# Delta-rule matrices at 64 columns a chunk instead of 128 a pair of chunks, in a 1-core Trainium2 kernel

## Chip, cores and metric

One NeuronCore of a Trainium2 chip runs the whole program. The metric is the device time of one execution in microseconds (us); smaller is better. TensorE is also called PE here, VectorE DVE, ScalarE ACT, GpSimd POOL, SyncE SP.

## What is computed

Two blocks of two layers each on 256 tokens of width 1024, all float32. The change lies in the second block, in its gated delta-rule branch. Its core, cut from the reference (CHUNK is 64, 8 heads, dk = dv = 128):

```python
qc, kc, vc, bc, gc = (chunks(t) for t in (q, k, v, beta, g))
gc = jnp.cumsum(gc, axis=-1)
incl = pos[:, None] >= pos[None, :]
strict = pos[:, None] > pos[None, :]
diff = gc[..., :, None] - gc[..., None, :]
decay = jnp.where(incl, jnp.exp(jnp.where(incl, diff, 0.0)), 0.0)
kb = kc * bc[..., None]
m = jnp.where(strict, jnp.einsum('bnhid,bnhjd->bnhij', kb, kc) * decay, 0.0)
rhs = jnp.concatenate([vc * bc[..., None], kb * jnp.exp(gc)[..., None]], axis=-1)
sol = lax.linalg.triangular_solve(m, rhs, left_side=True, lower=True, unit_diagonal=True)
u, w = sol[..., :dv], sol[..., dv:]
a_qk = jnp.einsum('bnhid,bnhjd->bnhij', qc, kc) * decay

def step(state, xs):
    qd, kd, a, uu, ww, cd = xs
    v_new = uu - ww @ state
    o = qd @ state + a @ v_new
    state = state * cd + kd.T @ v_new
    return state, o
```

(The last function is shown with its einsums as products.) Everything else, the other branches, the gates, the feed-forward layers and the first block, is as before in both kernels.

## The kernel before

**The stream.** All weights pass through one stream (class Stream). SP loads them in 1 MB chunks, ACT rounds a half chunk to its high part (L339), POOL subtracts to get the low part (L348), and PE multiplies in three passes (L147 to L149): high by high, low by high, high by low. With activations as the moving operand a pass is 128x128 weights by 256 columns. `main.pe(pe, pos)` issues the stream up to a position; one position is half of a half chunk, that is 12 passes.

**The branch work between.** Everything that is no stream is put on PE by hand, at a position of the stream. `places` (L1541) gives the steps of the delta rule their positions: most stand 1 position apart, some 2. Each engine goes through the same list of steps in its own order and waits on semaphores. The branch is done in two halves of four heads (`hf`), in each of the two layers, so each step occurs four times. Around it DVE does the short convolutions of the next projections (L1384) in the first half, and rotations (L1582 to L1585) in the second.

**The squares.** The 256 tokens are four chunks of 64. Before the change, two chunks of a head make one 128x128 square (tt = 0, 1 names the pair), block-diagonal after masking, so 4 heads x 2 pairs = 8 squares (NP) make one tile of 128x8x128 each: `e` (decays), `es`, `at` (query by key), `mt` (the matrix m, turned), `ti` (the inverse, turned), `t` (the inverse), `y`. Several share one place in memory. In the records a tile goes by the first name at its place: `y` shows as `es`, `t` as `e`, `w` as `kb`, `u` as `vb`.

**The steps**, in order, for one half of the heads:
- spread: `spread` (L1670) puts the row of g for each head on all 128 partitions by a product with 8-row weights, 256 columns (L1672); DVE takes the difference with the token's own g into `e` (L2205), ACT takes the exponential. `spread_e` and, later, `beta` spread two more rows.
- k0, k1, v0, v1: turns of k and v (L1678), read by DVE into `kb`, `kd`, `vb`.
- q0, q1, g0, g1: `gram` (L1684) makes the products of q and k, and of k and k, 4 per step; DVE masks them into `at` and `mt`, and begins the inverse in `ti` (L2252 to L2256).
- lower0, lower1: PE turns the 8 squares of `ti` (L1732), ACT copies them into `t` (L1980).
- y1, c1 to y5, c5: the inverse by doubling. `y` is 8 products mt x t (L1739), masked by DVE with the level's mask (L2275). `c` is 8 products ti x y into yd (L1748, not in level 5) and 8 products y x ti into cp (L1749); DVE subtracts them from `ti` (L2282) and `t` (L2284). The 8 squares go in two groups g of four, each with its own PSUM bank, wait and semaphore.
- solved: u = ti x vb (L1756) and w = kb x ti (L1757), 8 products each, copied by DVE (L2290) and ACT (L1985).
- w0, o0 to w3, o3: the scan over the four chunks (L1774, L1785, L1791, L1794), in which weights of 64 columns or 64 rows already occur.

Elsewhere in the kernel, products with operands on one half of the partitions stand in L565 (first block: 64x64 weights, four groups that alternate between the two halves of partitions, in and out), L1815 (index scores: 64-row weights, heads that alternate between the halves), L534 (64-column weights, outputs that alternate) and L1606 (turns of 8 rows: 8 moving columns).

Of the kernel before, what the change touches and what calls it, by code (L numbers as in the profile page):

```python
# [56 lines left out]
def columns(spec):  # L57
    at, out = 0, {}
    for name, n in spec:
# [10 lines left out]
                   ("chunk_causal", 2 * 256), ("perm128", 128), ("freq", 2), ("levels", 6 * 128), ("upper", 128),  # L70
                   ("strict", 128), ("level0T", 128),
# [6 lines left out]
def constants():  # L78
# [40 lines left out]
    i, j = p[:, None], p[None, :]  # L119
    lev = [((i // (2 * b) == j // (2 * b)) & (i // b > j // b)) for b in (1, 2, 4, 8, 16, 32)]  # L120
    put("levels", np.stack(lev, 1).astype(np.float64))
    put("level0T", lev[0].T.astype(np.float64))
    same = i // CH == j // CH
    put("upper", (same & (j >= i)).astype(np.float64))
    put("strict", (same & (j > i)).astype(np.float64))
# [937 lines left out]
NP = 8  # L1063
LAYOUT_2 = (["sm"] + [f"{n}{i}" for h in range(2) for n in "qkvz" for i in (2 * h, 2 * h + 1)]
# [256 lines left out]
class Mixer2:  # L1321
# [342 lines left out]
    def prepare_pe(self, pe, hf):  # L1664
# [28 lines left out]
        spread(m["rowq"][:, 1, :], 0).then_inc(*sig.up("spread_g", l, hf))  # L1693
# [23 lines left out]
        spread(m["rowq"][:, 0, :], 2).then_inc(*sig.up("spread_b", l, hf))  # L1717
# [5 lines left out]
    def solve_pe(self, pe, hf):  # L1723
# [27 lines left out]
        main.pe(pe, self.step_at(hf, "solved"))  # L1751
        for g in range(2):
            pe.wait_ge(*sig.at("kept", l, hf, g, 5))
            for n in range(4 * g, 4 * g + 4):
                c = slice((n % 4) * P, (n % 4 + 1) * P)
                pe.matmul(yd[g][:, c], h["ti"][:, n, :], h["vb"][:, n, :], start=True, stop=True)  # L1756
                mm = pe.matmul(cp[g][:, c], h["kb"][:, n, :], h["ti"][:, n, :], start=True, stop=True)  # L1757
            mm.then_inc(*sig.up("solved", l, hf, g))

    def scan_pe(self, pe, hf, key_sum):  # L1760
# [4 lines left out]
        for c in range(NCH):  # L1765
# [27 lines left out]
            for hh in range(4):  # L1793
                mm = pe.matmul(op[r, hh * P:(hh + 1) * P], h["at"][r, tt * 4 + hh, r], h["vn"][r, hh, :],  # L1794
# [175 lines left out]
    def chain_act(self, act, hf, key_log):  # L1970
# [6 lines left out]
        for g in range(2):  # L1977
            main.act(act, self.step_at(hf, f"lower{g}"))
            act.wait_ge(*sig.at("begun_turned", l, hf, g))
            act.activation(h["t"][:, 4 * g:4 * g + 4, :], bank[g][:, :].rearrange("p (n i) -> p n i", n=4), ACT.Copy  # L1980
                           ).then_inc(*sig.up("t_begun", l, hf, g))
# [211 lines left out]
    def prepare_dve(self, dve, hf, unit_key):  # L2193
# [9 lines left out]
        for hh in range(4):  # L2203
            for tt in range(TT):
                ins = dve.tensor_scalar(h["e"][:, tt * 4 + hh, :], bank[hh // 2][:, (hh % 2) * T + tt * P:(hh % 2) * T + (tt + 1) * P],  # L2205
# [15 lines left out]

        for tt in range(TT):
# [11 lines left out]
        step(dve.tensor_tensor(h["e"][:, :, :], h["e"][:, :, :], K("upper").unsqueeze(1).to_broadcast([P, NP, P]), ALU.mult))  # L2234
        for tt in range(TT):
# [3 lines left out]
            dve.tensor_tensor(h["at"][:, pr, :], heads(tt), h["e"][:, pr, :], ALU.mult).then_inc(*sig.up("at_made", l, hf, tt))  # L2239
        step(dve.tensor_tensor(h["es"][:, :, :], h["e"][:, :, :], K("strict").unsqueeze(1).to_broadcast([P, NP, P]), ALU.mult))  # L2240
# [3 lines left out]
        for i in range(2):  # L2244
            ins = dve.tensor_tensor(es[:, 2 * i:2 * i + 2, :, :], es[:, 2 * i:2 * i + 2, :, :],
                                    bank[2 + i][:, :].rearrange("p (hh tt i) -> p hh tt i", hh=2, tt=TT), ALU.mult)
        step(ins)
        for tt in range(TT):
# [3 lines left out]
            dve.tensor_tensor(h["mt"][:, pr, :], heads(tt), h["es"][:, pr, :], ALU.mult).then_inc(*sig.up("mt_made", l, hf, tt))  # L2252
            dve.wait_ge(*sig.at("mt_made", l, hf, tt))
            step(dve.tensor_tensor(h["ti"][:, pr, :], h["mt"][:, pr, :], K("level0T").unsqueeze(1).to_broadcast([P, 4, P]),
                                   ALU.mult))
            dve.tensor_tensor(h["ti"][:, pr, :], K("ident").unsqueeze(1).to_broadcast([P, 4, P]), h["ti"][:, pr, :],  # L2256
                              ALU.subtract).then_inc(*sig.up("begun", l, hf, tt))

    def solve_dve(self, dve, hf):
# [3 lines left out]
        ident = K("ident").unsqueeze(1).to_broadcast([P, 4, P])  # L2263
        lev = K("levels").rearrange("p (l i) -> p l i", l=6)

        def four(b):
            return bank[b][:, :].rearrange("p (n i) -> p n i", n=4)
# [435 lines left out]
```

## Time and profile before

| | us |
|---|---|
| median of 3 runs | 2276.24 |
| lowest, highest | 2274.07, 2278.8 |
| the profiled execution | 2277.58 |
| its span, first to last instruction | 2275.8 |

Over the span, VectorE is busy 955.9 us, ScalarE 1073.0, GpSimd 1498.6, and the mean granted clock of TensorE is 0.972 of full speed. TensorE has 15336 passes and as many weight loads. The page gives for each engine the busy time, its share and the number of instructions; the timeline lists instructions in order, merged where the same ones follow each other.

### The profile page before, as it was taken

How to read it: one execution, taken by the hardware profiler on the slowest of the kernel's cores; microseconds unless marked ns; L12 is line 12 of the kernel's file. 1: busy time of each engine (PE TensorE's matmuls, PEld its weight loads, DVE VectorE, ACT ScalarE, POOL GpSimd, SP SyncE). 2: the span in 40 equal slices, each digit the busy share in tenths (PEclk: the TensorE clock that was granted, in tenths of full speed). 3: DMA queues.
4: the chain of work that ended last, by engine and by line, in shares of the span. 5: the costliest groups of instructions: out<-in, count | busy, mean ns of one | idle time of the engine just before them, and what ended most of it. 6: DMA issues, size and time to landing. Idle time of an engine off the chain costs nothing.

```text
span 2275.8 us, 35984 instructions
## 1 busy us (share of the span) xinstructions
PE 2163.2 (95%) x15336; PEld 2001.3 (88%) x15336; DVE 955.9 (42%) x1484; ACT 1073.0 (47%) x1517; POOL 1498.6 (66%) x632
## 2 busy tenths in 40 slices
PE   8989989899969899999999899998999999999998
PEld 7789978799959888989999899898889899998998
DVE  4353256442375537477112211456374681123112
ACT  4555555555545352255444444473441454544444
POOL 6679877698846234356778688663243566786886
PEclk9999999999989999999999999999999999999999
DMA  8345544355524113134445455442131344454553
GB/s 338 132 146 204 185 139 161 117 180 187 184 84 147 60 71 106 64 128 167 151 164 185 148 185 185 156 145 90 56 112 56 130 148 149 157 182 150 184 185 133
DMA packets 47183, 333.05 MB, mean 146 GB/s; under 512 B 5168, under 2 KB 5552, under 8 KB 7856
## 3 DMA queue, kind: packets, MB, share of 16 engines
q1 hardware_dynamic: 47024, 330.76, 41.9%
q8 instruction: 121, 1.98, 0.4%
q14 instruction: 38, 0.31, 0.0%
HBM read 329.69 MB, written 1.05 MB: 145 GB/s over the span
## 4 chain that ended last, share of the span: by engine, by line
PE 62%; DVE 8%; issue 1%; ACT 1%; POOL 0%; DVEq 0%; ACTq 0%
PE bank L147 14%; PE bank L149 14%; PE bank L148 14%; PE y L147 2%; PE y L149 2%; PE y L148 2%; PE bank L1749 2%; PE bank L1748 1%; PE bank L1739 1%; DVE conv L1384 1%; PE bank L1672 1%; PE bank L1794 1%; PE bank L1791 1%; PE bank L1774 1%; DVE sq L1583 1%
## 5 line engine op out<-in xcount | busy, mean ns | idle before, releaser
L348 POOL TENSOR_TENSOR w_lo<-w_raw,w_hi 128x1024 fp32r<-128x1024 f32 x602 | 1463.0, 2437 | 759.7 <-ACT w_hi L339 759.6
L339 ACT ACTIVATE w_hi<-w_raw 128x1024 fp32r<-128x1024 f32 x602 | 635.7, 1059 | 1009.4 <-PE bank L149 838.9
L147 PE MATMUL bank<-x_hi,w_hi 128*128 128x256 f32 x2960 | 876.6, 296 | 21.6 <-POOL w_lo L348 17.1
L148 PE MATMUL bank<-x_lo,w_hi 128*128 128x256 f32 x2960 | 848.4, 287 | 0.0
L149 PE MATMUL bank<-x_hi,w_lo 128*128 128x256 f32 x2960 | 848.3, 287 | 0.0
L147 PEld LDWEIGHTS bank<-x_hi,w_hi 128*128 128x128 f32 x2960 | 579.1, 196 | 44.9 <-issue 24.4
L148 PEld LDWEIGHTS bank<-x_lo,w_hi 128*128 128x128 f32 x2960 | 579.0, 196 | 10.5 <-issue 8.6
L149 PEld LDWEIGHTS bank<-x_hi,w_lo 128*128 128x128 f32 x2960 | 578.4, 195 | 0.0
L876 DVE SCALAR_TENSOR_TENSOR conv<-bank,par_sb,conv 128x254 f32<-128x254 f32 (+1 forms) x176 | 76.8, 478 | 240.1 <-ACT conv L864 238.6
L1246 DVE TENSOR_TENSOR hid_lo<-hid,hid_hi 128x512 fp32r<-128x512 f32 x22 | 45.1, 2048 | 241.2 <-ACT hid_hi L1241 241.2
L147 PE MATMUL y<-w_hi,hid_hi 128*128 128x512 f32 x352 | 139.9, 397 | 3.3 <-DVE hid_lo L898 3.3
L149 PE MATMUL y<-w_hi,hid_lo 128*128 128x512 f32 x352 | 138.9, 395 | 0.0
L148 PE MATMUL y<-w_lo,hid_hi 128*128 128x512 f32 x352 | 138.9, 395 | 0.0
L1384 DVE SCALAR_TENSOR_TENSOR conv<-bank,par_sb,conv 128x255 f32<-128x255 f32 (+1 forms) x144 | 62.6, 477 | 63.8 <-ACT conv L1375 62.1
L147 PEld LDWEIGHTS y<-w_hi,hid_hi 128*128 128x128 f32 x352 | 66.3, 188 | 19.2 <-DVE hid_lo L898 5.4
L149 PEld LDWEIGHTS y<-w_hi,hid_lo 128*128 128x128 f32 x352 | 66.2, 188 | 15.7
L148 PEld LDWEIGHTS y<-w_lo,hid_hi 128*128 128x128 f32 x352 | 66.2, 188 | 13.8
L1491 DVE SCALAR_TENSOR_TENSOR gate<-gate,bank 128x512 f32<-128x512 f32 x16 | 11.0, 688 | 130.5 <-PE bank L149 130.5
L1749 PE MATMUL bank<-ti,es 128*128 128x128 f32 x320 | 61.0, 290 | 4.1 <-DVE es L2275 4.1
L1748 PE MATMUL bank<-es,ti 128*128 128x128 f32 x256 | 51.8, 286 | 7.0 <-DVE es L2275 7.0
L1749 PEld LDWEIGHTS bank<-ti,es 128*128 128x128 f32 x320 | 49.6, 205 | 4.5 <-DVE es L2275 4.5
L2347 DVE SCALAR_TENSOR_TENSOR sc<-index,tokq,sc 128x128 f32<-128x128 f32 (+1 forms) x28 | 52.6, 1878 | 1.0
(397 smaller groups left out, 3243.6 us busy)
## 6 DMA issues: line engine op xcount, KB each, us to landing
w_raw<-w SPq DMA_DIRECT2D x300, 1024.0 KB, 4.8
ln_rows<-ln_rows SPq DMA_DIRECT2D x4, 1024.0 KB, 7.2
mem_tok<-mem SPq DMA_DIRECT2D x2, 1024.0 KB, 4.9
const_sb<-const SPq DMA_DIRECT2D x1, 1536.0 KB, 9.3
par_sb<-par SPq DMA_DIRECT2D x2, 553.5 KB, 10.7
xn<-xT SPq DMA_DIRECT2D x1, 1024.0 KB, 4.9
w_raw<-w SPq DMA_DIRECT2D x2, 512.0 KB, 5.4
x_tok<-x SPq DMA_DIRECT2D x1, 1024.0 KB, 7.2
```

What stands on the lines that cost most here:

```text
L147: pe.matmul(out, lhs[0], rhs[0], start=start, stop=False, skip_group_check=skip)
L148: pe.matmul(out, lhs[0], rhs[1], start=False, stop=False, skip_group_check=skip)
L149: return pe.matmul(out, lhs[1], rhs[0], start=False, stop=stop, skip_group_check=skip)
L339: act.activation(self.hi[:, h % HALVES, :], self.raw[:, n % RAWS, i * HW:(i + 1) * HW], ACT.Copy).then_inc(*sig.up("high", h))
L348: pool.tensor_tensor(self.lo[:, h % HALVES, :], self.raw[:, n % RAWS, i * HW:(i + 1) * HW], self.hi[:, h % HALVES, :].bitcast(F32), ALU.su ...
L876: ins = dve.scalar_tensor_tensor(cb[:, j, tap:T], view[:, j, 0:T - tap], taps[:, 2 - tap, c0 + j:c0 + j + 1], cb[:, j, tap:T], ALU.mult, A ...
L1246: dve.tensor_tensor(net.hs2[1][:, 2 * (i % 3):2 * (i % 3) + 2, :], m["hid"][:, i % 2, :, :], net.hs2[0][:, 2 * (i % 3):2 * (i % 3) + 2, :] ...
L1384: ins = dve.scalar_tensor_tensor(cb[:, j, tap:T], two(b)[:, j, 0:T - tap], taps[:, 3 - tap, c0 + j:c0 + j + 1], cb[:, j, tap:T], ALU.mult, ...
L1583: net.dve_chain.step(dve.tensor_tensor(raw, raw, cos.unsqueeze(1).to_broadcast([P, w, T]), ALU.mult))
L1748: pe.matmul(yd[g][:, c], h["ti"][:, n, :], h["y"][:, n, :], start=True, stop=True)
L1749: mm = pe.matmul(cp[g][:, c], h["y"][:, n, :], h["ti"][:, n, :], start=True, stop=True)
L2347: ins = dve.scalar_tensor_tensor(sc, m["r"][qt][:, (h % 2) * 4 + h // 2, :], m["tokq"][:, qt, 4, h:h + 1], mask if h == 0 else sc, ALU.mul ...
```

## The change

The squares become 64 columns wide: partition p of a square is token p of the pair of chunks, column j is token j of the same chunk. So chunk 0 lies on partitions 0 to 63, chunk 1 on 64 to 127, and the zero blocks are no longer stored. Each product of squares becomes two of 64x64 by 64 columns, one with operands and output on partitions 0 to 63, the other on 64 to 127. The spreads of g and beta write the chunk's own columns only; gram makes one 64x64 product per chunk from 128-row operands; `lower` multiplies by the identity instead of a transpose; `u` and `w` are made per chunk, `w` with one PSUM bank per chunk and one semaphore for all of it. DVE and ACT handle 256 columns for four squares instead of 512. Constants shrink accordingly, with an `eye` of 64 columns more.

```diff
-        spread(m["rowq"][:, 1, :], 0).then_inc(*sig.up("spread_g", l, hf))
+        spread_chunks(m["rowq"][:, 1, :], 0).then_inc(*sig.up("spread_g", l, hf))
...
+        def spread_chunks(rows, b):
+            chunks = rows.rearrange("p (t c i) -> p c t i", t=TT, c=2)
+            for hh in range(4):
+                for c in range(2):
+                    mm = pe.matmul(bank[b][c * CH:(c + 1) * CH, hh * P:(hh + 1) * P], sel[0:8, 4 * hf + hh, c * CH:(c + 1) * CH],
+                                   chunks[:, c, :, :], start=True, stop=True)
+            return mm
...
         def gram(other, tt):
-            c = slice(tt * P, (tt + 1) * P)
             for hh in range(4):
-                mm = pe.matmul(bank[tt][:, hh * P:(hh + 1) * P], k[:, hh, c], other[:, hh, c], start=True, stop=True)
+                for c in range(2):
+                    r = slice(tt * P + c * CH, tt * P + (c + 1) * CH)
+                    mm = pe.matmul(bank[tt][c * CH:(c + 1) * CH, hh * CH:(hh + 1) * CH], k[:, hh, r], other[:, hh, r],
+                                   start=True, stop=True)
...
+        both = [slice(c * CH, (c + 1) * CH) for c in range(2)]
...
-                mm = pe.transpose(yd[g][:, (n % 4) * P:(n % 4 + 1) * P], h["ti"][:, n, :], K("ident"))
+                for r in both:
+                    mm = pe.matmul(yd[g][r, (n % 4) * CH:(n % 4 + 1) * CH], h["ti"][r, n, :], K("ident")[r, r], start=True, stop=True)
...
-                    mm = pe.matmul(yd[g][:, (n % 4) * P:(n % 4 + 1) * P], h["mt"][:, n, :], h["t"][:, n, :],
-                                   start=True, stop=True)
+                    for r in both:
+                        mm = pe.matmul(yd[g][r, (n % 4) * CH:(n % 4 + 1) * CH], h["mt"][r, n, :], h["t"][r, n, :],
+                                       start=True, stop=True)
...
                     if lv < 5:
-                        pe.matmul(yd[g][:, c], h["ti"][:, n, :], h["y"][:, n, :], start=True, stop=True)
-                    mm = pe.matmul(cp[g][:, c], h["y"][:, n, :], h["ti"][:, n, :], start=True, stop=True)
+                        for r in both:
+                            pe.matmul(yd[g][r, c], h["ti"][r, n, :], h["y"][r, n, :], start=True, stop=True)
+                    for r in both:
+                        mm = pe.matmul(cp[g][r, c], h["y"][r, n, :], h["ti"][r, n, :], start=True, stop=True)
...
             for n in range(4 * g, 4 * g + 4):
-                c = slice((n % 4) * P, (n % 4 + 1) * P)
-                pe.matmul(yd[g][:, c], h["ti"][:, n, :], h["vb"][:, n, :], start=True, stop=True)
-                mm = pe.matmul(cp[g][:, c], h["kb"][:, n, :], h["ti"][:, n, :], start=True, stop=True)
+                for r in both:
+                    mm = pe.matmul(yd[g][r, (n % 4) * P:(n % 4 + 1) * P], h["ti"][r, n, :], h["vb"][r, n, :], start=True, stop=True)
             mm.then_inc(*sig.up("solved", l, hf, g))
+        for n in range(NP):
+            for c, r in enumerate(both):
+                mm = pe.matmul(cp[c][:, n * CH:(n + 1) * CH], h["kb"][r, n, :], h["ti"][r, n, :], start=True, stop=True)
+        mm.then_inc(*sig.up("w_solved", l, hf))
...
-        for g in range(2):
-            act.wait_ge(*sig.at("solved", l, hf, g))
-            act.activation(h["w"][:, 4 * g:4 * g + 4, :], bank[2 + g][:, :].rearrange("p (n i) -> p n i", n=4), ACT.Copy
-                           ).then_inc(*sig.up("w_kept", l, hf, g))
+        act.wait_ge(*sig.at("w_solved", l, hf))
+        for c in range(2):
+            act.activation(h["w"][:, :, c * CH:(c + 1) * CH], bank[2 + c][:, :].rearrange("p (n i) -> p n i", n=NP), ACT.Copy
+                           ).then_inc(*sig.up("w_kept", l, hf, c))
...
-                dve.tensor_tensor(h["y"][:, pr, :], four(g), lev[:, lv:lv + 1, :].to_broadcast([P, 4, P]), ALU.mult
+                dve.tensor_tensor(h["y"][:, pr, :], four(g), lev[:, lv:lv + 1, :].to_broadcast([P, 4, CH]), ALU.mult
```

## Rows read from the trace of the kernel before

**Rows 1.** The page, part 1: busy us (share of the span) xinstructions of each engine

```profile
PE 2163.2 (95%) x15336; PEld 2001.3 (88%) x15336; DVE 955.9 (42%) x1484; ACT 1073.0 (47%) x1517; POOL 1498.6 (66%) x632
```

**Rows 2.** Timeline of PE, solve: start us, us, engine line op out<-in xcount

```profile
762.06 1.95 PE L1739 MATMUL bank<-e,mt 128*128 128x128 f32 x16
...
763.96 0.28 PE L148 MATMUL bank<-x_lo,w_hi 128*128 128x256 f32 x1
...
765.28 0.38 PE L1748 MATMUL bank<-es,ti 128*128 128x128 f32 x2
...
768.97 0.28 PE L148 MATMUL bank<-x_lo,w_hi 128*128 128x256 f32 x1
```

**Rows 3.** Timeline of PE: spread, turning of four squares, gram

```profile
708.62 0.28 PE L149 MATMUL bank<-x_hi,w_lo 128*128 128x256 f32 x1
708.83 1.99 PE L1672 MATMUL bank<-rowq,const_sb 8*128 8x256 f32 x8
...
710.97 0.28 PE L148 MATMUL bank<-x_lo,w_hi 128*128 128x256 f32 x1
...
711.81 0.41 PE L149 MATMUL bank<-x_hi,w_lo 128*128 128x256 f32 x1
...
725.45 0.60 PE L1678 MATMUL bank<-const_sb,v_set 128*128 128x128 f32 x4
...
726.01 0.28 PE L148 MATMUL bank<-x_lo,w_hi 128*128 128x256 f32 x1
...
731.53 1.05 PE L1684 MATMUL bank<-q_set,k_set 128*128 128x128 f32 x8
...
732.54 0.28 PE L148 MATMUL bank<-x_lo,w_hi 128*128 128x256 f32 x1
```

**Rows 4.** Timeline of PE: products in part tiles of the array

```profile
44.13 0.28 PE L149 MATMUL bank<-x_hi,w_lo 128*128 128x256 f32 x1
44.34 1.08 PE L565 MATMUL pool_bank<-pooled,par_sb 64*64 64x256 f32 x8
...
45.57 0.28 PE L148 MATMUL bank<-x_lo,w_hi 128*128 128x256 f32 x1
...
825.57 1.16 PE L1785 MATMUL bank<-v_new,kd 64*128 64x128 f32 x8
...
827.67 1.08 PE L1794 MATMUL bank<-v_new,at 64*64 64x128 f32 x8
...
828.91 0.28 PE L148 MATMUL bank<-x_lo,w_hi 128*128 128x256 f32 x1
...
988.71 0.39 PE L149 MATMUL bank<-w_hi,x_lo 128*128 128x512 f32 x1
989.03 1.16 PE L1815 MATMUL bank<-ik,iq 64*128 64x128 f32 x16
...
990.46 0.39 PE L148 MATMUL bank<-w_lo,x_hi 128*128 128x512 f32 x1
```

**Rows 5.** Timeline of PEld, the weight loads: two short bursts

```profile
88.50 0.42 PEld L534 LDWEIGHTS o<-pt,abv 128*64 128x64 f32 x8 [0.37 <-issue]
...
685.21 0.69 PEld L1606 LDWEIGHTS bank<-const_sb,rowq 8*128 8x128 f32 x10
```

**Rows 6.** Weight loads of two lines: xcount, duration ns min/median/max, first and last start

```profile
L1794 PEld LDWEIGHTS bank<-v_new,at x128: 129/133/227, 815.6 to 1786.1; 64*64 64x64 f32 x128
...
L1815 PEld LDWEIGHTS index<-ik,iq x32: 182/187/187, 1009.1 to 1820.7; 64*128 64x128 f32 x32
```

**Rows 7.** Timelines of PE and DVE: waits [idle us <-what ended it] and masks

```profile
748.62 0.66 PE L1732 MATMUL bank<-const_sb,ti 128*128 128x128 f32 x4 [3.09 <-DVE ti L2256]
...
772.36 2.69 DVE L1384 SCALAR_TENSOR_TENSOR conv<-bank,par_sb,conv 128x255 f32<-128x255 f32 x6 [2.03 <-ACT conv L1375]
774.97 1.28 DVE L2275 TENSOR_TENSOR es<-bank,const_sb 128x512 f32<-128x512 f32 x2
...
775.70 0.49 PE L1748 MATMUL bank<-es,ti 128*128 128x128 f32 x2 [2.04 <-DVE es L2275]
```

More of the change, by code:

```diff
@@ L69 @@
 CC, NCC = columns([("ident", 128), ("perm64", 128), ("select", 8 * 128), ("ln_eps", 1), ("ones", 128), ("eps", 1),
-                   ("chunk_causal", 2 * 256), ("perm128", 128), ("freq", 2), ("levels", 6 * 128), ("upper", 128),
-                   ("strict", 128), ("level0T", 128),
+                   ("chunk_causal", 2 * 256), ("perm128", 128), ("freq", 2), ("levels", 6 * CH), ("upper", CH),
+                   ("strict", CH), ("level0T", CH), ("eye", CH),
                    ("causal", 2 * 256), ("band", 2 * 4 * 256), ("cos", 256), ("sin", 256)])
@@ L118, in constants @@
     put("freq", f)
-    i, j = p[:, None], p[None, :]
+    i, j = p[:, None] % CH, np.arange(CH)[None, :]
     lev = [((i // (2 * b) == j // (2 * b)) & (i // b > j // b)) for b in (1, 2, 4, 8, 16, 32)]
     put("levels", np.stack(lev, 1).astype(np.float64))
[L122 to L125, printed above, removed]
+    put("level0T", ((i // 2 == j // 2) & (j > i)).astype(np.float64))
+    put("upper", (j >= i).astype(np.float64))
+    put("strict", (j > i).astype(np.float64))
+    put("eye", (j == i).astype(np.float64))
     sel = np.zeros((8, 8, P))
@@ L1063 @@
 NP = 8
+SQUARES = ("at", "mt", "ti", "e", "t", "es", "y")
 LAYOUT_2 = (["sm"] + [f"{n}{i}" for h in range(2) for n in "qkvz" for i in (2 * h, 2 * h + 1)]
@@ L1716, in prepare_pe @@
         pe.wait_ge(*sig.at("v_read", l, hf, 1))
-        spread(m["rowq"][:, 0, :], 2).then_inc(*sig.up("spread_b", l, hf))
+        spread_chunks(m["rowq"][:, 0, :], 2).then_inc(*sig.up("spread_b", l, hf))
         for tt in range(TT):
@@ L1793, in scan_pe @@
             for hh in range(4):
-                mm = pe.matmul(op[r, hh * P:(hh + 1) * P], h["at"][r, tt * 4 + hh, r], h["vn"][r, hh, :],
+                mm = pe.matmul(op[r, hh * P:(hh + 1) * P], h["at"][r, tt * 4 + hh, :], h["vn"][r, hh, :],
                                start=False, stop=True, skip_group_check=True)
@@ L2220, in heads, with squares @@
             return bank[b][:, :].rearrange("p (h d) -> p h d", h=4)
+        def squares(b):
+            return bank[b][:, 0:T].rearrange("p (h i) -> p h i", h=4)
         for tt in range(TT):
@@ L2233, in prepare_dve @@
         dve.wait_ge(*sig.at("decay_made", l, hf))
-        step(dve.tensor_tensor(h["e"][:, :, :], h["e"][:, :, :], K("upper").unsqueeze(1).to_broadcast([P, NP, P]), ALU.mult))
+        step(dve.tensor_tensor(h["e"][:, :, :], h["e"][:, :, :], K("upper").unsqueeze(1).to_broadcast([P, NP, CH]), ALU.mult))
         for tt in range(TT):
@@ L2238, in prepare_dve @@
             pr = slice(tt * 4, tt * 4 + 4)
-            dve.tensor_tensor(h["at"][:, pr, :], heads(tt), h["e"][:, pr, :], ALU.mult).then_inc(*sig.up("at_made", l, hf, tt))
-        step(dve.tensor_tensor(h["es"][:, :, :], h["e"][:, :, :], K("strict").unsqueeze(1).to_broadcast([P, NP, P]), ALU.mult))
+            dve.tensor_tensor(h["at"][:, pr, :], squares(tt), h["e"][:, pr, :], ALU.mult).then_inc(*sig.up("at_made", l, hf, tt))
+        step(dve.tensor_tensor(h["es"][:, :, :], h["e"][:, :, :], K("strict").unsqueeze(1).to_broadcast([P, NP, CH]), ALU.mult))
         main.dve(dve, self.step_at(hf, "beta"))
@@ L2243, in prepare_dve @@
         es = h["es"][:, :, :].rearrange("p (tt hh) i -> p hh tt i", tt=TT)
[L2244 to L2247, printed above, removed]
+        step(dve.tensor_tensor(es, es, bank[2][:, :].rearrange("p (hh tt i) -> p hh tt i", hh=4, tt=TT), ALU.mult))
         for tt in range(TT):
@@ L2262, in solve_dve @@
         step, h = net.dve_chain.step, m["half"]
[L2263 removed]
         lev = K("levels").rearrange("p (l i) -> p l i", l=6)
         def four(b):
[L2267 removed]
+            return bank[b][:, 0:T].rearrange("p (n i) -> p n i", n=4)
         main.dve(dve, self.step_at(hf, "lower1"))
@@ L2289, in solve_dve @@
             dve.wait_ge(*sig.at("solved", l, hf, g))
-            dve.tensor_copy(h["u"][:, 4 * g:4 * g + 4, :], four(g)).then_inc(*sig.up("u_kept", l, hf, g))
+            dve.tensor_copy(h["u"][:, 4 * g:4 * g + 4, :], bank[g][:, :].rearrange("p (n i) -> p n i", n=4)).then_inc(*sig.up("u_kept", l, hf, g))
     def scan_dve(self, dve, hf, unit_key):
@@ L2496, in second_memory @@
                                         ("es", "y"))):
-            h[n] = place(n, 32 + 4 * i, [P, NP, P])[:, :, :]
-            if other:
+            h[n] = place(n, 32 + 4 * i, [P, NP, CH if n in SQUARES else P])[:, :, :]
+            if other in SQUARES:
                 h[other] = h[n]
+            elif other:
+                h[other] = place(other, 32 + 4 * i, [P, NP, P])[:, :, :]
         h["o"] = h["u"]
```

12 lines of the change are left out of this document (6 added, 6 removed).

## The prediction

> **What bounds the kernel now.** I read the page's busy shares first: TensorE is busy 95% of the span, every other engine 66% or less [rows 1]. So a microsecond is won only where TensorE's own line of work gets shorter. The timeline of TensorE around the solve says how that line is built: between two pieces of the weight stream (12 passes of 128x256, one every 0.12 us, 1.43 us a piece) stands one block of delta-rule products, and the stream goes on when the block is through. A block is paid in full. It also shows that one matmul of the text is two passes in the records: a `y` block of 8 products stands as x16 [rows 2].
>
> I price a block by what it delays: start of the second stream pass behind it, less the start of the last stream pass before it, less two pitches of 0.12 (the second, because the first one behind a block starts late). Where the row before is not shown, no gap stood there, and one pitch is taken off the block's own start.
> - `y`: 763.96 - 762.06 - 0.12 = 1.78 us, or some 0.106 a pass and the rest at its ends [rows 2]
> - `c` with both products: 768.97 - 765.28 - 0.12 = 3.57 us [rows 2]; `solved` has the same 32 passes
> - turning of four 128x128 squares: 726.01 - 725.45 - 0.12 = 0.44; gram: 732.54 - 731.53 - 0.12 = 0.89; spreading rows to four heads: 710.97 - 708.62 - 0.24 = 2.11 [rows 3]
>
> **What small tiles cost, from the same trace.** The array is already used in part tiles elsewhere. Eight passes of 64x64 weights, all in one corner, 128 columns: 828.91 - 827.67 - 0.12 = 1.12, and 0.09 of gap ahead as in the next case, so 1.21. At 0.106 a pass that is 0.85 of streaming and 0.36 of entering and leaving the part-tile layout [rows 4]. Eight passes of 64x64 weights that alternate between opposite corners, 256 columns each: 45.57 - 44.13 - 0.24 = 1.20. The eight 256-column passes of the spread, which share one tile, took 2.11 [rows 3, 4]. Less the 0.36 that is 0.105 a pass, though 256 columns take a pass twice 0.106. So two corners do run at once. The third case alternates two row halves with 128-column weights and 128 moving columns: 990.46 - 988.71 - 0.46 (two pitches of 0.23 there) = 1.29 for 16 passes, less 0.36 is 0.058 a pass [rows 4].
>
> **The new passes.** The squares become 64x64 per chunk, each product of 128 splits in two of 64x64x64 in opposite corners. There are twice as many passes, each with 64 moving columns, half of those of the 0.058 row, and with 64-column weights, also half. If both scale, the pitch is 0.029; I take p = 0.030. No row shows a 64-column pass, so p is bounded: below by 64 columns at the 0.105/256 of the corner row, 0.026; above by 0.0615, the pitch of weight loads in front of 8-column passes ((0.69 - 0.137)/9, of ten loads of 0.137 [rows 5]). I take the low end because that 8-column case has one tile only and loads 128 columns, and the alternating rows are nearer in kind.
>
> **Block by block**, four preparations (two layers, two halves of the heads):
> - `y` 20 blocks and the fifth `c` 4 blocks, 16 passes become 32: 0.36 + 32 x 0.030 = 1.32, saves 0.46 x 24 = 11.0
> - `c` of levels 1 to 4, 16 blocks, 32 passes become 64: 0.36 + 64 x 0.030 = 2.28, saves 1.29 x 16 = 20.6
> - spread of g and of beta, 8 blocks: 8 passes of 256 columns become 16 of 128 that alternate column halves: 0.36 + 16 x 0.058 = 1.29, saves 0.82 x 8 = 6.5 (the third spread, `spread_e`, stays)
> - gram, 16 blocks, 8 passes become 16: 0.84 for 0.89, saves 0.8 in all
> - `lower`, 8 blocks: four one-pass transposes become 16 passes: 0.84 for 0.44, costs 3.2
> - `solved`, 4 blocks: `u` is 32 passes with 128 columns, `w` is 32 with 64-column streams but 128-column weights, whose load I price like the 0.058 row; the two are different layouts, so 2 x 0.36 + 64 x 0.058 = 4.43, costs 0.9 x 4 = 3.5
> Sum: 32.2 us saved.
>
> **Off TensorE.** VectorE's operations on squares halve from 512 to 256 columns. A 512-column one lasts 0.69 with a pitch near 0.6 [rows 7]; I take 0.38 (between half and all of 0.69). This lies beside the stream except where TensorE waits. In the first half of the heads six `c` blocks wait for their mask, 2.04 us the longest, since a convolution of 2.69 us stands before it [rows 7]. There TensorE resumes when the mask is done, so the 0.46 of the shorter `y` is lost and only 0.3 of the shorter mask is kept: -1 in all. The four waits before the second `lower` (3.09 the longest [rows 7]) have three operations on squares ahead of them, which shrink by 0.3 each: between 0 and all of the 3.09, taken 0.7 each, +3. The clock: 1.1 us after the spread's 8-row passes the stream's pass goes from 0.28 to 0.41 with no idle time before it, that is from 2.4 to 1.2 GHz [rows 3]. Three spreads of the twelve do this, each some 16 passes at 0.21 instead of 0.12, about 1.6 us. One of the three changes, the others stand shortly behind one that does; worth 0 to 5, taken 2. `w` is copied only when all of it is solved: two ScalarE copies of 0.6 after the block, while two stream pieces (2.9) stand ahead of the first reader: nothing. Behind the wait on ScalarE stands the next rounding of the stream, which before stood behind the second copy as well. Without that cover it would be 1.2 x 4. The 1312 more passes on TensorE's queue (384 + 512 + 128 + 64 + 96 + 128) and as many loads are priced within p. The smaller constants are loaded in the first block: nothing.
>
> Total 32.2 - 1 + 3 + 2 = 36 us. The profiled execution took 2277.58 (span 2275.8), so it would be 2241; the median of the runs is 1.3 lower, so 2240 there.
>
> The Trainium skill has a rule against this change. TensorEngine Tiling (Array Packing), section Performance Considerations, says a matmul has about 60 cycles of overhead whatever its columns and that no tiling should be taken from a dimension that is already small. TensorE: Matmul & The Clock Gate, section Back-to-back issue gap, puts the floor at about 25 ns, or at about 62 ns a MATMUL where the sequencer decodes in software. An estimate by the first leaves p where it is; by the second the sum would be the slow rival below. The trace cannot decide: its 8-column row stands at 61.5 ns, and no block of it asks for a pass in less than 53 over its whole length.
>
> **The rivals.** The saving by p alone is 36 + 2176 x (0.030 - p), as 768 + 1024 + 256 + 128 = 2176 passes have 64 columns. It crosses zero at p = 0.0465.
> 1. Slower: the short passes of a pair don't overlap as the long ones do. If a corner's load (64 columns more cost a load 187 - 133 = 54 ns [rows 6]) and its stream of 53 take turns, p = 0.053: 14 us lost, 2290. With a floor of 0.0615: 32 lost, 2308. For it speaks the 8-column row. Against it: in the 128-column case load (about 107) and stream (107) have the same proportion and overlap fully.
> 2. In between: p = 0.040, the pitch of eight 64-column loads in a burst ((0.42 - 0.137)/7 [rows 5]): 14 saved, 2262. It was eight loads only, with 128-column passes behind them, so it is an upper bound for what a burst can do as well.
> 3. The blocks fill too little of the array and the clock falls behind each of the 16 long `c`, as behind a spread: 16 x 1.6 = 26 back, 2266. Against it: three part-tile blocks in a row, 825.57 to 828.68, leave the stream's passes at 0.28 behind them [rows 4].
> 4. The blocks shrink, but masks come later than the stream piece covers. Behind `y` VectorE has 1.43 us for about 0.7; a rotation of 2 us stands ahead of some masks of the second half. Some 20 blocks x 0.5: 2250.
>
> **How the numbers follow.** Forecast 0.49, slower 0.17, in between 0.18, clock 0.05, late masks 0.06, something that makes no difference 0.05. A measurement tells about 0.2%, 4.6 us, from no change. Faster is 0.49 + 0.18 + 0.05 + 0.06 = 0.78, less a little for their upper ends: 0.77; within 0.2%: 0.06; slower: 0.17. The range runs from p = 0.026 with every side gain (36 + 9 + 5: 2226), a little lower since several are open, to just past no change, which leaves the slow rival out: 2224 to 2280.
>
> **What would show it.** Right: `y` blocks of about 1.3, `c` blocks of about 2.3 us between the same stream passes, pairs of passes every 0.06, spreads at 1.3, waits at the six masks 0.2 longer. Wrong: `c` blocks of 3.5 or more (rival 1), stream passes of 0.41 behind them (rival 3), new waits for VectorE (rival 4), or `lower` and `solved` dearer than priced, which shows 0.36 to be too small.

## The result and the profile after

| | before | after |
|---|---|---|
| median, us | 2276.09 | 2223.45 |
| lowest, highest | 2274.07, 2278.8 | 2222.2, 2224.56 |
| span of the profiled execution | 2275.8 | 2220.4 |
| passes on TensorE | 15336 | 16648 |

The change makes the kernel faster: the ratio of the times is 0.9768, 95% interval 0.9751 to 0.9785, or 52.6 us. The forecast was 2240, a gain of 36. The sign and the main mechanism were right, the gain was too small by 17 us, and the range (2224 to 2280) missed the median by 0.55 us.

The page of after, part 1, answers to [rows 1]. There are 1312 more passes, TensorE is 47 us less busy and VectorE 57, whose operations on squares are half as long; ScalarE and GpSimd hardly change:

```profile
PE 2116.4 (95%) x16648; PEld 1944.2 (88%) x16648; DVE 899.2 (40%) x1480; ACT 1068.7 (48%) x1517; POOL 1496.3 (67%) x632
```

The timeline of TensorE in after, a `y` block and a `c` block, against [rows 2] (start us, duration us, then engine, line, operation and tiles):

```profile
753.96 0.28 PE L149 MATMUL bank<-x_hi,w_lo 128*128 128x256 f32 x1
754.16 1.15 PE L1753 MATMUL bank<-e,mt 64*64 64x64 f32 x32
...
755.47 0.28 PE L148 MATMUL bank<-x_lo,w_hi 128*128 128x256 f32 x1
...
756.66 0.28 PE L149 MATMUL bank<-x_hi,w_lo 128*128 128x256 f32 x1
756.87 0.33 PE L1763 MATMUL bank<-es,ti 64*64 64x64 f32 x4
757.04 0.28 PE L1765 MATMUL bank<-ti,es 64*64 64x64 f32 x4
...
759.11 0.28 PE L148 MATMUL bank<-x_lo,w_hi 128*128 128x256 f32 x1
```

By the prediction's way of pricing, `y` costs 755.47 - 753.96 - 0.24 = 1.27 us (1.78 before) and `c` 759.11 - 756.66 - 0.24 = 2.21 (3.57 before; the other `c` blocks after have 2.20). The two differ by 32 passes and 0.94 us, so a pass is 0.029 and what is left of either block, its two ends, is 0.34. Behind the first, groups of four passes start every 0.117 us, the same 0.029.

The other blocks, against [rows 3] and the forecast's price of `solved`:

```profile
708.18 0.28 PE L149 MATMUL bank<-x_hi,w_lo 128*128 128x256 f32 x1
708.39 1.09 PE L1681 MATMUL bank<-rowq,const_sb 8*64 8x128 f32 x16
...
709.63 0.28 PE L148 MATMUL bank<-x_lo,w_hi 128*128 128x256 f32 x1
...
869.20 0.28 PE L149 MATMUL bank<-x_hi,w_lo 128*128 128x256 f32 x1
869.41 0.69 PE L1694 MATMUL bank<-k_set 128*64 128x64 f32 x16
...
870.25 0.28 PE L148 MATMUL bank<-x_lo,w_hi 128*128 128x256 f32 x1
...
910.91 1.96 PE L1772 MATMUL bank<-vb,ti 64*64 64x128 f32 x32
912.81 2.00 PE L1776 MATMUL bank<-ti,kb 64*128 64x64 f32 x32
914.74 1.12 PE L1568 MATMUL bank<-sk,const_sb 128*128 128x512 f32 x2
```

The spread is 1.21, gram 0.81, and `lower` too, within 0.01 (16 passes as in gram, row at 741.79 below); `u` takes 1.90 us for 32 passes and `w` 1.93, 0.06 a pass each.

The waits of TensorE in after (what it waited for: us in total, times, longest) have no line for `lower`, which in before is four waits with 10.6 us in all. Those at the masks have grown, from 11.1 us in six waits to 13.7, and from 2.04 to 2.28 in the longest case [rows 7]:

```profile
PE bank L1763 <- DVE es L2293: 9.1, 4, 2.3
...
PE bank L1765 <- DVE es L2293: 4.6, 2, 2.3
```

### The profile page after: what moved, and what is told of

The parts are those of the page before. It is cut to its first block, busy times and chain, and to the rows that moved or that the text cites. A ratio compares the mean times of both kernels' runs of the same rounds, so it can differ in the third digit from the quotient of the medians.

```text
span 2220.4 us, 38604 instructions
## 1 busy us (share of the span) xinstructions
PE 2116.4 (95%) x16648; PEld 1944.2 (88%) x16648; DVE 899.2 (40%) x1480; ACT 1068.7 (48%) x1517; POOL 1496.3 (67%) x632
## 3 DMA queue, kind: packets, MB, share of 16 engines
q8 instruction: 131, 2.15, 0.4%
## 4 chain that ended last, share of the span: by engine, by line
PE 65%; DVE 5%; issue 1%; ACT 1%; POOL 0%; DVEq 0%; ACTq 0%
PE bank L147 15%; PE bank L148 14%; PE bank L149 14%; PE y L147 2%; PE y L149 2%; PE y L148 2%; PE bank L1765 1%; PE bank L1568 1%; PE bank L1763 1%; DVE conv L1385 1%; PE bank L1813 1%; PE bank L1810 1%; PE bank L1753 1%; PE bank L1793 1%; PE bank L1594 1%
## 5 line engine op out<-in xcount | busy, mean ns | idle before, releaser
L2365 DVE SCALAR_TENSOR_TENSOR sc<-index,tokq,sc 128x128 f32<-128x128 f32 (+1 forms) x28 | 52.6, 1878 | 1.0
L147 PE MATMUL bank<-w_hi,x_hi 128*128 128x512 f32 x128 | 52.4, 409 | 0.0
L148 PE MATMUL bank<-w_lo,x_hi 128*128 128x512 f32 x128 | 50.0, 390 | 0.0
L149 PE MATMUL bank<-w_hi,x_lo 128*128 128x512 f32 x128 | 49.9, 390 | 0.0
```

The costliest lines, as they stand in the source:

```text
L147: pe.matmul(out, lhs[0], rhs[0], start=start, stop=False, skip_group_check=skip)
L148: pe.matmul(out, lhs[0], rhs[1], start=False, stop=False, skip_group_check=skip)
L149: return pe.matmul(out, lhs[1], rhs[0], start=False, stop=stop, skip_group_check=skip)
L2365: ins = dve.scalar_tensor_tensor(sc, m["r"][qt][:, (h % 2) * 4 + h // 2, :], m["tokq"][:, qt, 4, h:h + 1], mask if h == 0 else sc, ALU.mul ...
```

## Experiments

The time of after on its own chip was 0.9768 of before. The runs below stand beside runs of before (2274.4 to 2276.5 us); I compare them with after's 2223.5, which is uncertain by some 2 us from chip to chip.

### What makes a pass cost 0.029

**Both products of a pair in one corner.**

```diff
-                    for r in both:
-                        mm = pe.matmul(yd[g][r, (n % 4) * CH:(n % 4 + 1) * CH], h["mt"][r, n, :], h["t"][r, n, :],
+                    r = both[0]
+                    for i in range(2):
+                        mm = pe.matmul(yd[g][r, i * T + (n % 4) * CH:i * T + (n % 4 + 1) * CH], h["mt"][r, n, :], h["t"][r, n, :],
```

(and the same in `c`)

> Made from the kernel after. In the y and c products of the five levels, both products of a matrix are done in the corner of chunk 0, the second into the spare upper columns of the same bank, so the number, shape and size of the passes is as after, and no pass has a neighbour in the other corner. It leaves out the squares of chunk 1 (computed again for chunk 0 instead), so its time is that of the same count of passes without opposite corners. Theory: 0.029 us a pass is what two passes in opposite corners beside each other give, and in one corner a pass takes 0.05 to 0.06 us; the y block goes from 1.27 to about 2.05 us, c from 2.20 to about 3.75, and with 20 y blocks, 16 c blocks and 4 short ones the time rises by 35 to 50 us over after, to about 2258 to 2273 us (ratio to before 0.992 to 0.999). Rival: a pass of 64 columns costs 0.03 us wherever it stands; blocks and time stay (2223 us, ratio 0.977).

Measured: 2276.78 us, ratio 1.0002 [0.9981, 1.0022]. Timeline of TensorE, a `y` block:

```profile
775.08 0.28 PE L149 MATMUL bank<-x_hi,w_lo 128*128 128x256 f32 x1
775.29 2.08 PE L1754 MATMUL bank<-e,mt 64*64 64x64 f32 x32
...
777.52 0.28 PE L148 MATMUL bank<-x_lo,w_hi 128*128 128x256 f32 x1
```

That is 2.20 us, and a `c` block with no wait is 4.06: a pass takes (4.06 - 2.20) / 32 = 0.058, exactly twice 0.029, with the same 0.34 at the ends. The blocks are dearer by 20 x 0.93 + 16 x 1.85 + 4 x 0.93 = 52 us. In the profiled execution 5.6 of it is covered by the waits at the masks, which shrink to 8.1, and some 4 by less time at 1.2 GHz (31 us against 39 in after, summed as told under the waits before `lower`, half of it lost). 3.0 are added by a wait for VectorE at L513, at 377 us in the first block, which the edit doesn't touch: 45, and its span is 45.5 longer than after's. That execution is among the fastest of ten, which lie from 2266.9 to 2291.5; why they spread so far is open. Their median is 53 over after, just past my 35 to 50. So, by the prices of the blocks, the two corners at work side by side are worth 52 us in `y` and `c`, as much as the whole change gains. Twice as many passes of half the columns, one after the other, are dearer than the passes of before (2.20 against 1.78, 4.06 against 3.57, 18 us in all); in this kernel that is made up by what else the change gains.

**Corner by corner.** Same products, `for r in both` outside the loop over n.

> Made from the kernel after, same computation. In the y and c products the order within a group is corner by corner (4 or 8 products in one corner, then as many in the other) instead of alternating with each product. Theory A: only direct neighbours in opposite corners overlap, so that a run of 8 or 16 passes in one corner costs 0.05 to 0.06 us a pass; then the time rises as far as with one corner alone, by 35 to 50 us (ratio 0.992 to 0.999). Theory B: the instruction queue lets a run in one corner go beside the run in the other, or the price isn't one of neighbours; then the blocks stay at 1.27 and 2.20 us within 0.1 and the time within 5 us of after (ratio 0.975 to 0.979). I hold A at 2 in 3.

Measured: 2252.88 us, ratio 0.9896 [0.9878, 0.9914], between the two theories. Timeline, a `y` block:

```profile
761.76 0.28 PE L149 MATMUL bank<-x_hi,w_lo 128*128 128x256 f32 x1
761.97 1.54 PE L1753 MATMUL bank<-e,mt 64*64 64x64 f32 x32
...
763.66 0.28 PE L148 MATMUL bank<-x_lo,w_hi 128*128 128x256 f32 x1
```

1.66 us, 0.54 under one corner's 2.20; `c` is 3.53, 0.53 under 4.06. In `y` the runs in one corner are 8 passes long, in `c` 16, and both blocks have three switches. So the saving goes with the switches, about 0.18 us or three passes at each, and not with the length of the runs. The starts of the single passes in the trace show it: at each switch three passes of the new run begin within 0.006 us of one of the old run, and behind the first pass of the block the others stand 0.052 to 0.059 apart. In after every second pass begins 0.007 us behind the one before it. Alternating with every product is what fills both corners all the time. Neither theory was right as put: the loss is 29 us, under A's 35 to 50.

**Which part of "opposite corner" counts.** Two kernels, in which neighbouring products differ in only one direction:

```diff
-                        mm = pe.matmul(yd[g][r, (n % 4) * CH:(n % 4 + 1) * CH], h["mt"][r, n, :], h["t"][r, n, :],
+                        mm = pe.matmul(yd[g][r, (n % 4) * CH:(n % 4 + 1) * CH], h["mt"][both[0], n, :], h["t"][both[0], n, :],
```

> Made from the kernel after. In the y and c products both products of a pair take their operands from the 64 rows of chunk 0 and write to the two halves of the columns in turn, so that neighbours differ in their columns of the array and not in their rows. It leaves out the products of chunk 1 (those of chunk 0 stand in their place); count and size of the passes are as after. Theory S: passes overlap only where rows and columns both differ; then a pass costs 0.058 us as with one corner: y block 2.20, c block 4.06, time 2270 to 2280 us (ratio 0.998 to 1.002). Theory T: other columns are enough; y 1.27, c 2.20, time 2220 to 2226 us (ratio 0.975 to 0.979). I hold S at 6 in 10.

```diff
-                    for r in both:
-                        mm = pe.matmul(yd[g][r, (n % 4) * CH:(n % 4 + 1) * CH], h["mt"][r, n, :], h["t"][r, n, :],
+                    c = slice((n % 4) * CH, (n % 4 + 1) * CH)
+                    for r, to in zip(both, (yd, cp)):
+                        mm = pe.matmul(to[g][both[0], c], h["mt"][r, n, :], h["t"][r, n, :], start=True, stop=True)
```

> Made from the kernel after. In the y and c products the two products of a pair take their operands from the rows of chunk 0 and of chunk 1 in turn, but both write to the 64 columns of chunk 0 (into different banks), so that neighbours differ in their rows of the array and not in their columns. It leaves out that the products of chunk 1 reach chunk 1's partitions; count and size of the passes are as after. Where neighbours share the rows and differ in the columns, the time was that of after (2221 us, y block 1.27), where they share both it was 2277 us (y block 2.20). Theory C: what overlaps are passes in different columns of the array; here none do, y 2.20, c 4.06, time 2265 to 2285 us (ratio 0.996 to 1.004). Theory D: any other corner is enough; y 1.27, c 2.20, 2220 to 2226 us (ratio 0.975 to 0.979). The gram in the trace of after (passes over all 128 rows, columns in turn, 0.81 us for 16) fits both. I hold C at 6 in 10.

(`c` is changed in the same way in both.) Measured: 2221.4 us, ratio 0.9766 [0.9748, 0.9784], and 2222.41, ratio 0.9764 [0.9742, 0.9785]. I was wrong on both. A `y` block with shared rows, then one with shared columns:

```profile
762.67 0.28 PE L149 MATMUL bank<-x_hi,w_lo 128*128 128x256 f32 x1
762.88 1.15 PE L1753 MATMUL bank<-e,mt 64*64 64x64 f32 x32
...
764.18 0.28 PE L148 MATMUL bank<-x_lo,w_hi 128*128 128x256 f32 x1
```

```profile
754.30 0.28 PE L149 MATMUL bank<-x_hi,w_lo 128*128 128x256 f32 x1
754.51 1.15 PE L1754 MATMUL bank<-e,mt 64*64 64x64 f32 x32
...
755.81 0.28 PE L148 MATMUL bank<-x_lo,w_hi 128*128 128x256 f32 x1
```

Both are 1.27, as in after. Any other quarter of the array will do. After's own gram says the same with tiles of 128 rows by 64 columns: 16 passes in 0.81 us, (0.81 - 0.34) / 16 = 0.029. The Trainium skill has it (TensorEngine Tiling (Array Packing), Key Properties): tiles work independently and different ones load and multiply at once, and a change of the tiling mode drains the engine. The traces agree with the first, and the 0.34 us at the ends of each block fits the second, though no run separates it.

### Where the waits before `lower` went

In before, VectorE's second operation on the new `ti` is slow in the first half of the heads. Timelines of VectorE and GpSimd of before (the wait of TensorE is in [rows 7]), then of VectorE, GpSimd and TensorE of after:

```profile
745.13 0.69 DVE L2254 TENSOR_TENSOR ti<-mt,const_sb 128x512 f32<-128x512 f32 x1
745.85 2.71 DVE L2256 TENSOR_TENSOR ti<-const_sb,ti 128x512 f32<-128x512 f32 x1
745.41 2.61 POOL L348 TENSOR_TENSOR w_lo<-w_raw,w_hi 128x1024 fp32r<-128x1024 f32 x1 [1.88 <-ACT w_hi L339]
```

```profile
740.40 0.41 DVE L2271 TENSOR_TENSOR mt<-bank,es 128x256 f32<-128x256 f32 x1
740.85 0.42 DVE L2273 TENSOR_TENSOR ti<-mt,const_sb 128x256 f32<-128x256 f32 x1
741.31 0.43 DVE L2275 TENSOR_TENSOR ti<-const_sb,ti 128x256 f32<-128x256 f32 x1
741.40 2.58 POOL L348 TENSOR_TENSOR w_lo<-w_raw,w_hi 128x1024 fp32r<-128x1024 f32 x1 [1.87 <-ACT w_hi L339]
...
741.79 0.68 PE L1745 MATMUL bank<-const_sb,ti 64*64 64x64 f32 x16
```

In before the operation began 0.44 us after the stream's subtraction on GpSimd and ended 0.54 us after it: it stood until GpSimd was done. In after all three operations have begun before GpSimd does, the last by only 0.09 us, and it takes its normal 0.43. The three got shorter by 0.8 us in all, and TensorE got back 3.09.

**Each preparing operation twice, in after.**

```diff
+            dve.tensor_tensor(h["spare"], squares(tt), h["es"][:, pr, :], ALU.mult)
             dve.tensor_tensor(h["mt"][:, pr, :], squares(tt), h["es"][:, pr, :], ALU.mult)...
```

(and so for the two on `ti`)

> Made from the kernel after, same result. The three operations by which VectorE makes mt and ti out of a gram (128 x 256 elements each, 0.42 us) are each issued twice, the first time into a spare tile, so that they take as long as before. Theory: the 2.2 to 3.1 us for which TensorE waited ahead of the second of the turned-over products in each half before, and that are gone after, are decided by when these operations start against the GpSimd operation of 2.6 us beside them; they come back in at least two of the four halves, and the time rises by 5 to 12 us (2228 to 2235 us, ratio 0.979 to 0.982), with idle of 2 to 3 us ahead of that block in the trace. Rival: the waits went for another reason (the blocks of TensorE around them moved); the time rises by less than 3 us and no such idle is seen.

Measured: 2236.61 us, ratio 0.9824 [0.9809, 0.9838], 13.2 over after, a microsecond over my upper end. Timelines of VectorE, GpSimd and TensorE:

```profile
743.15 0.42 DVE L2275 TENSOR_TENSOR spare<-mt,const_sb 128x256 f32<-128x256 f32 x1
743.50 2.56 DVE L2276 TENSOR_TENSOR ti<-mt,const_sb 128x256 f32<-128x256 f32 x1
743.37 2.41 POOL L348 TENSOR_TENSOR w_lo<-w_raw,w_hi 128x1024 fp32r<-128x1024 f32 x1 [1.88 <-ACT w_hi L339]
...
746.91 0.75 PE L1745 MATMUL bank<-const_sb,ti 64*64 64x64 f32 x16 [3.13 <-DVE ti L2278]
```

The short operation takes 2.56 us as soon as it starts behind GpSimd's. All four waits are back: 3.13, 1.99, 3.13 and 1.99, 10.2 in all. The other 2.9 is no more than the clock can account for: summed in windows of 2 us over the two stretches with the delta rule (680 to 1060 and 1440 to 1860), TensorE's time at 1.2 GHz is 51 us, as in before, against 39 in after. That is 12 more, of which at most half is lost, and those at the masks are 0.9 shorter.

**Short preparing operations, in before.**

```diff
-            dve.tensor_tensor(h["mt"][:, pr, :], heads(tt), h["es"][:, pr, :], ALU.mult)...
+            dve.tensor_tensor(h["mt"][:, pr, 0:CH], heads(tt)[:, :, 0:CH], h["es"][:, pr, 0:CH], ALU.mult)...
```

(and so for the two on `ti`, the other columns set to zero ahead of `beta`)

> Made from the kernel before. The three operations of VectorE that make mt and ti out of a gram are done on 64 of the 128 columns of each chunk (128 x 256 elements, as after), the other columns are set to zero ahead of them; everything else is as before. It leaves out chunk 1's columns of mt and ti, so its time is that of before with a short preparation. Theory: what is late for the second of the turned-over products in each half is VectorE's operation on tiles in SBUF that starts behind a GpSimd operation and then lasts as long as that one; with short operations none or few start behind it, as after, and the waits of 3.09, 2.22, 3.09 and 2.22 us go: the time falls by 8 to 13 us (2263 to 2268 us, ratio 0.9943 to 0.9965). Rival: only the shorter operations count, some 0.7 us a place (my forecast): 3 us less (ratio 0.9985), and the waits stay at 1.5 to 2.4 us.

Measured: 2267.19 us, ratio 0.9969 [0.9958, 0.9980], 7.2 us less. Timeline of TensorE, the second turn of either half of the heads:

```profile
745.02 0.66 PE L1732 MATMUL bank<-const_sb,ti 128*128 128x128 f32 x4 [0.27 <-DVE ti L2258]
...
887.96 0.66 PE L1732 MATMUL bank<-const_sb,ti 128*128 128x128 f32 x4 [1.74 <-DVE ti L2258]
```

The waits are 0.27, 1.74, 0.27, 1.74, 4.0 us in all for 10.6; I had expected all four to go, and 8 us at least. So the theory holds for the first half of the heads, where 2.8 of the 3.09 go with 0.27 saved in each of three operations. In the second half only 0.48 of 2.22 goes: an operation on `ti` still begins behind GpSimd's (885.29, 2.15 us long). In after that wait is gone too. There VectorE also stands behind GpSimd (871.61, 2.17 us long), but GpSimd's operation began 2.4 us before the first `lower`, where in before it began 1.4 us after it. That is a matter of where the shortened blocks put the stream against VectorE, read from the traces and not put to a test of its own. It was luck that it came out well here; no length of an operation would have told.

The Trainium skill (GPSIMD Engine Reference, Key points) lists contention between GpSimd and VectorE where a VectorE instruction has two inputs in SBUF. The traces agree, and show the contention to be a full stop for an operation that begins behind GpSimd's. The row at 741.31 above shows that one which begins ahead of it isn't held. Nor is an operation with one input in a PSUM bank. In before, 18 of the 40 masks (L2275) begin while the subtraction runs and take 0.68 to 0.69 us, as the others do. VectorE and GpSimd of before:

```profile
764.04 0.69 DVE L2275 TENSOR_TENSOR es<-bank,const_sb 128x512 f32<-128x512 f32 x1 [0.20 <-PE bank L1739]
763.45 2.39 POOL L348 TENSOR_TENSOR w_lo<-w_raw,w_hi 128x1024 fp32r<-128x1024 f32 x1 [8.14 <-ACT w_hi L339]
```

### The spread

```diff
-        spread_chunks(m["rowq"][:, 1, :], 0)...
+        spread(m["rowq"][:, 1, :], 0)...
```

(and for beta)

> Made from the kernel after, same result. The rows g and beta are spread over the partitions as before (eight passes of 256 columns into two banks for each, where after has them in four pairs of passes of half the work), and VectorE picks the columns it needs. Theory: the block costs 2.11 us against 1.21, eight of them, 7.2 us on TensorE's path, and up to 3 us more or less from the clock, that falls behind one of them: 2229 to 2234 us (ratio 0.979 to 0.982). Rival: the spreads lie beside a wait somewhere and their length is hidden: within 2 us of after.

Measured: 2236.37 us, ratio 0.9826 [0.9809, 0.9843], 12.9 over after. For the partitions of chunk 1 the edit takes the columns of chunk 0, with the same operations, so the text's "same result" is not so; the work is that of the full one. The block is back at 2.11, eight times 0.90 is the 7.2 expected. The other 5.7 is more than my 3 for the clock, and the clock has it. TensorE's windows in the second half of layer 0 (busy us, passes, granted clock, DMA share, GB/s), after and then this kernel:

```profile
840.00:870.00 30.00, 30.00 (x266) 0.94 0.37 121
```

```profile
840.00:870.00 30.00, 30.00 (x215) 0.89 0.31 106
```

In all the time at 1.2 GHz in the two stretches is 55 us against 39. Half of the 15 more, 7.6, is a little more than the 5.7.

### The masks ahead of the convolution

**In after.**

```diff
-            main.dve(dve, self.step_at(hf, f"y{lv}"))
             for g in range(2):
                 pr = slice(4 * g, 4 * g + 4)
                 dve.wait_ge(*sig.at("lower", l, hf, g, lv))
                 dve.tensor_tensor(h["y"][:, pr, :], ...)
+            main.dve(dve, self.step_at(hf, f"y{lv}"))
```

> Made from the kernel after, same result. In each level VectorE does the two masks behind the y products first and then the main line's own operation of that step (the convolution of 2.5 us that the masks stood behind), where after does it ahead of them. Theory: the idle of 2.28 us ahead of the c products in six of the levels goes (13.7 us in all), unless the main line's stream then waits for its own operation instead; with that about half is kept: the time falls by 6 to 14 us and up to 3 us more for a clock that doesn't fall (2206 to 2217 us, ratio 0.969 to 0.974). Rival: the stream behind the block needs that operation at once and the wait only changes its place; the time is within 3 us of after (ratio 0.976 to 0.978).

Measured: 2198.88 us, ratio 0.9662 [0.9646, 0.9678]. This is 24.6 us faster than after and beats both kernels. VectorE in after, then with the masks first:

```profile
762.50 2.69 DVE L1385 SCALAR_TENSOR_TENSOR conv<-bank,par_sb,conv 128x255 f32<-128x255 f32 x6 [2.74 <-ACT conv L1376]
765.10 0.75 DVE L2293 TENSOR_TENSOR es<-bank,const_sb 128x256 f32<-128x256 f32 x2
```

```profile
762.30 0.89 DVE L2292 TENSOR_TENSOR es<-bank,const_sb 128x256 f32<-128x256 f32 x2 [1.49 <-PE bank L1753]
763.55 2.68 DVE L1385 SCALAR_TENSOR_TENSOR conv<-bank,par_sb,conv 128x255 f32<-128x255 f32 x6 [0.37 <-ACT conv L1376]
```

The six waits of 2.28 are gone, 13.7 us, and nothing waits for the convolution. The gain is larger than the upper end I gave, since the clock gives as much again. TensorE's windows with the clock as third number, after, then masks first:

```profile
750.00:800.00 50.00, 43.70 (x634) 0.91 0.21 72
800.00:840.00 40.00, 40.00 (x278) 0.91 0.18 63
```

```profile
750.00:800.00 50.00, 48.26 (x707) 1.00 0.26 86
800.00:840.00 40.00, 40.00 (x301) 0.99 0.30 101
```

In the two stretches the time at 1.2 GHz falls from 39 to 13 us, worth 13. Together 27. From the first spread of a layer to its last scan product the trace is 14.5 us shorter in the first layer and 11.6 in the second, 26 in all, for 24.6 between the medians. (The profiled execution is only 17.9 shorter in its whole span. It was the longest of the four and lost 4.9 before the delta rule began, 3.0 of them in the same wait at L513, which this edit doesn't touch either.)

**In before**, the same edit.

> Made from the kernel before, same result: in each level the masks are done ahead of the main line's own operation of that step on VectorE. The same edit took 24.6 us off the kernel after (2223.5 to 2198.9). Theory: here the idle ahead of the c products is 1.4 to 2.0 us in six levels, 11.1 us in all, and its going gives 11 us and 4 to 8 us more from a clock that then falls less often: 2257 to 2262 us (ratio 0.992 to 0.994), so that the change is worth 57 to 63 us where no masks are late. Rival: the edit gives the same 24 us here (2252, ratio 0.989), and the change's worth doesn't depend on the late masks (53 us).

Measured: 2262.36 us, ratio 0.9940 [0.9923, 0.9957], 12.0 less. The 11.1 us of waits go and the time at 1.2 GHz falls from 51 to 41 us, worth 5. That makes 16 for 12 between the medians; the rest is open. (The span of the profiled execution, the fastest of its four, is 17.7 shorter, with the wait of 3.0 at L513 in it.) With the masks first on both sides the change is worth 2262.4 - 2198.9 = 63.5 us, just over my 57 to 63; the late masks take 11 of it away.

## Why the prediction was right or wrong

**The price of a block: right.** p is 0.029 where I took 0.030, the ends are 0.34 where I took 0.36. `y` is 1.27 for 1.32, `c` 2.20 for 2.28, the spread 1.21 for 1.29, gram 0.81 for 0.84, `lower` 0.81 for 0.84. `solved` is 4.02 where the clock doesn't fall (so in the kernel with the masks first), for 4.43. Nearly every block was cheaper by 0.03 to 0.08 us and `solved` by 0.4, and there are 76 of them. By these prices the work saved is 10.2 + 2.0 (`y`, fifth `c`) + 21.9 (`c`) + 7.2 (spread) + 1.3 (gram) - 3.0 (`lower`) - 1.8 (`solved`) = 37.8 us where the sum has 32.2. That is 5.6 of the 17 that are missing.

**Why it was right.** I scaled the 0.058 of passes that alternate between rows [rows 4] by one half. The runs show the reason: a pass of 64 columns costs 0.058 where neighbours share a corner, a little over half of the 0.106 of a 128-column pass, and 0.029, half of that again, where they don't. I said opposite corners, but another row half or another column half does as well.

**The waits before the second `lower`: the step that failed.** I took 0.7 each, +3, between 0 and 3.09. All 10.6 us of them went, 7.6 more than forecast. The 3.09 was read as a chain of work that shrinks with its three operations. It was mostly one operation held up by GpSimd, and the duration of 2.71 beside a normal 0.69 stood in the trace of before. Short operations in before alone bring 6.6 of the 10.6; the other 4 came with the shift of the blocks, as far as the traces show.

**The waits at the masks: right for four, missed for two.** They are 13.7 us for 11.1, a loss of 2.6 where I took 1. Four of the six grew by 0.24 each, from 2.04 to 2.28, which is the 1. The first of each layer grew by 0.8 each, from 1.49 and 1.43. In before the `y` block ahead of it runs at 1.2 GHz behind the wait of 3.09, takes 2.47 us instead of 1.78, and so hides part of the mask's delay. With short preparing operations in before (the wait of 3.09 down to 0.27) that mask's wait is 2.03. So 1.6 of the 10.6 us won ahead of `lower` were lost again here.

**The clock: mis-sized.** I took 2, in 0 to 5. The time at 1.2 GHz in the two stretches went from 51 to 39 us, worth up to 5.9. These are single executions, and the kernel with shared rows, whose blocks are priced as after's, has 43. I looked at the spreads alone; after still has three falls behind spreads, all now behind the unchanged `spread_e`. The falls behind waits count as much, as the runs with waits put in or taken out show.

**The sum again:** 37.8 + 10.6 - 2.6 + 5.9 = 51.7 for 52.6 between the medians and 55.4 between the two spans. Of the 55.4, 1.8 lie behind the last row of the delta rule's layers, where nothing was changed. Some 2 us I can't place. Of the 17 us by which the forecast missed the medians, 7.6 are the waits before `lower`, 5.6 the prices and 3.9 the clock, less 1.6 for the masks; 1 stays open.

**The rivals.** Rivals 1 and 2 (dear short passes) are out: 0.029, no gap of 0.053. Even with `y` and `c` all in one corner, where the pass was 0.058, the time was that of before and not slower. The 0.0615 of the 8-column row of [rows 5] is no floor for these passes; it is near the 0.058 of passes that share a corner. Rival 3 (the clock behind each `c`): no fall behind a `c` that didn't wait. Rival 4 (late masks in the second half): no such wait appears.

The page of the Trainium skill that the prediction cites (TensorE: Matmul & The Clock Gate, Back-to-back issue gap) has about 25 ns or, decoded in software, about 62 ns a MATMUL. The first agrees with 0.029 a pass, the second does not, and the measurement decides. The other page of the Trainium skill (TensorEngine Tiling (Array Packing), Performance Considerations) has an overhead of about 60 cycles, as long as 60 columns. The prediction read that as a rule against the change, but the new passes have 64 columns, so it need not bind, and the kernel is 52 us faster.

**The range.** It was bounded below by p = 0.026 "with every side gain", and the measured time lay just below it. I had held 0 to 5 for the clock and one small number for four waits whose own bound of 12 us stood in the text: the low end should have taken in the 9 us between my +3 and that bound, 2217 or so. That is said in hindsight. The miss is half a microsecond, but the sum behind it was short by a third of the gain.

## What to carry to other kernels

When a block of small products is split for the array, let neighbouring products in the instruction order stand in different quarters of it, whichever; with runs of eight or sixteen in one quarter, 29 of the 52 us were lost. Before pricing a wait as a chain of work, compare each operation's duration with the same operation elsewhere: a VectorE operation with both inputs in SBUF that takes the length of a GpSimd operation beside it is held, and 0.3 us less in each operation ahead of it can be worth 3. And a wait on TensorE costs more than its own length: taking out 11.1 us of waits gave 5 us more by the clock, taking out 13.7 gave 13.

## What the runs showed of the hardware that was not expected

- Passes overlap across any two quarters of the array, also with shared rows or shared columns: 0.029 us a pass against 0.058. At a switch from a run in one quarter to a run in another, three passes start beside the old run (0.18 us saved).
- VectorE's operation with both inputs in SBUF stands still while GpSimd's 128x1024 subtraction runs, if it begins behind it: 2.56 us instead of 0.42, and 2.71 instead of 0.69. Begun 0.09 us ahead of it, it takes 0.43; with one input in PSUM it takes its 0.68 to 0.69 either way.
- Six waits of 2.28 us on TensorE brought with them 27 us at 1.2 GHz. Without them the clock in that stretch was 1.00 where it had been 0.91.
